# One step of a hybrid encoder layer: u in its own PSUM banks, the first sums of squares beside q and k, first scores behind a gate tile, two means ahead of the last chain

## The reference

```python
xn = rms_norm(x, g_mix)
h = xn @ w_in                       # [u | q | k | v | gate_a | gate_b]
gates = sigmoid(gates + b_gate)
y_pool = multiscale_pool(u)         # trailing windows 2/4/8/16, mean minus token, per-group map, scale
z = q k^T / 8                       # strictly causal
log_not = where(causal, log_sigmoid(-z), 0)
suffix = sum of log_not over the later keys
o = exp(log_sigmoid(z) + suffix) @ v          # stick-breaking, no softmax
x = x + (gate_a * (y_pool @ w_pool_up) + gate_b * (o @ w_sb_up)) @ w_out
x = x + square(relu(rms_norm(x) @ w_up)) @ w_down
x = x + sigmoid(rms_norm(x) @ w_ple_gate) * (p @ w_ple_proj)
y = rms_norm(x)                     # outputs also: k, v and the last 15 rows of u
```

## Time and profile before

| | |
|---|---|
| median of 3 runs | 793.26 us (792.95 to 793.46) |
| the profiled execution's own time | 793.77 us |
| its span | 791.9 us |
| PE busy | 773.7 us (98%) |
| DVE busy | 494.8 us (62%) |
| ACT busy | 381.5 us (48%) |
| POOL busy | 96.9 us (12%) |
| granted PE clock, mean | 0.996 |

### The profile page before, as it was taken

One profiled execution on the slowest core, in us unless ns is written; L12 is line 12 of the kernel. 1 busy time (PEld: TensorE's weight loads), 2 busy tenths in 40 slices (PEclk: granted clock), 3 DMA queues, 4 the chain that ended last, 5 costly groups with the idle time before them and its releaser, 6 DMA issues.

```text
span 791.9 us, 14329 instructions
## 1 busy us (share of the span) xinstructions
PE 773.7 (98%) x6050; PEld 765.2 (97%) x6050; DVE 494.8 (62%) x606; ACT 381.5 (48%) x443; POOL 96.9 (12%) x169
## 2 busy tenths in 40 slices
PE   8899999999999999999999999999999999999993
PEld 8899999999999899999999999999999999999993
DVE  5876566566566547787763367434763367677965
ACT  6554534535575443665641255213642155555643
POOL 1040140150150000020001100020001100100001
PEclk9999999999999999999999999999999999999998
DMA  7342231232221316786566847587575856826402
GB/s 236 99 125 74 70 120 53 82 105 56 98 90 55 107 54 206 240 202 178 179 171 168 202 160 206 139 188 183 158 192 145 204 171 180 195 82 161 119 1 113
DMA packets 33097, 110.18 MB, mean 139 GB/s; under 512 B 4496, under 2 KB 4496, under 8 KB 33040
## 3 DMA queue, kind: packets, MB, share of 16 engines
q1 hardware_dynamic: 24768, 84.72, 32.4%
q0 software_dynamic: 6016, 21.04, 14.9%
q10 hardware_dynamic: 2256, 3.60, 1.3%
HBM read 94.33 MB, written 4.52 MB: 125 GB/s over the span
## 4 chain that ended last, share of the span: by engine, by line
PE 90%; DVE 5%; ACT 2%; issue 1%; DMA 1%; SPq 1%; DVEq 0%; ACTq 0%
PE psum L1352 24%; PE psum L1061 19%; PE psum L1067 19%; PE psum L1064 19%; PE psum L1114 1%; DMA xt<-x_t 1%; PE psum L1042 1%; PE psum L1142 1%; PE psum L1043 1%; PE psum L1044 1%; PE psum L1140 1%; PE psum L1430 1%; PE psum L1102 1%; DVE work L1473 1%; PE psum L1101 1%
## 5 line engine op out<-in xcount | busy, mean ns | idle before, releaser
L699 ACT ACTIVATE w_hi<-raw_more 128x1024 fp32r<-128x1024 f32 x84 | 88.7, 1056 | 133.0 <-PE psum L1067 100.7
L1064 PE MATMUL psum<-b_lo,w_hi 128*128 128x272 f32 x688 | 142.0, 288 | 0.0
L1061 PE MATMUL psum<-b_hi,w_hi 128*128 128x272 f32 x672 | 139.3, 288 | 0.0
L1067 PE MATMUL psum<-b_hi,w_lo 128*128 128x272 f32 x672 | 138.8, 288 | 0.0
L1061 PE MATMUL psum<-a_hi,w_hi 128*128 128x272 f32 x576 | 120.8, 291 | 3.3 <-DVE a_lo L1462 1.2
L1456 DVE TENSOR_TENSOR w_lo<-raw_more,w_hi 128x1024 fp32r<-128x1024 f32 x84 | 102.2, 1222 | 34.6 <-ACT w_hi L699 34.3
L1067 PE MATMUL psum<-a_hi,w_lo 128*128 128x272 f32 x576 | 119.0, 288 | 0.0
L1064 PE MATMUL psum<-a_lo,w_hi 128*128 128x272 f32 x576 | 118.8, 288 | 0.0
L1352 PE MATMUL psum<-u_hi,w_hi 128*128 128x272 f32 x560 | 115.9, 288 | 0.2 <-ACT h_of L933 0.2
L1352 PE MATMUL psum<-u_hi,w_lo 128*128 128x272 f32 x560 | 115.7, 288 | 0.0
L1352 PE MATMUL psum<-u_lo,w_hi 128*128 128x272 f32 x560 | 115.5, 287 | 0.0
(11 more groups left out here) (245 smaller groups left out, 1010.3 us busy)
## 6 DMA issues: line engine op xcount, KB each, us to landing
raw_more<-w_tiles SPq DMA_DIRECT2D x84, 512.0 KB, 4.3
raw<-w_tiles SPq DMA_DIRECT2D x66, 512.0 KB, 3.5
raw_more<-w_tiles POOLq DMA_DIRECT2D x16, 512.0 KB, 6.7
raw_more<-raw_more POOLq DMA_DIRECT2D x14, 512.0 KB, 8.3
xt<-x_t SPq DMA_DIRECT2D x8, 272.0 KB, 6.2
y_t<-xt SPq DMA_DIRECT2D x8, 272.0 KB, 2.5
raw<-w_tiles POOLq DMA_DIRECT2D x4, 512.0 KB, 7.6
raw_more<-raw POOLq DMA_DIRECT2D x3, 512.0 KB, 6.4
```

What stands on the lines that cost most here:

```text
L699: act.activation(w_hi[:, t % W_RING, :, :].rearrange("p k c -> p (k c)"), src, ACT.Copy)\
L1061: pe.matmul(base[:, h, :], w_hi[:, s, wk, :], at(hi, k, h * HALF, (h + 1) * HALF), start=(opens and q == 0), stop=False, skip_group_check= ...
L1064: pe.matmul(base[:, h, :], w_hi[:, s, wk, :], at(lo, k, h * HALF, (h + 1) * HALF), start=False, stop=False, skip_group_check=True)
L1067: mm = pe.matmul(base[:, h, :], w_lo[:, s, wk, :], at(hi, k, h * HALF, (h + 1) * HALF), start=False, stop=(closes and q == len(ks) - 1), s ...
```

## The change

Pair 0 is written in a new order. `result_slot` gives u (tile 3) slot 3, banks 6 and 7. The sums of squares are made behind the fourth step of tile 2, not the second, as four matmuls of 136 columns in place of two of 272, into unused columns of banks 0 to 3. TensorE's order in pair 0 becomes tiles 0, 1, 2, 3, 4, scores of head 0, transposes of v, tiles 5 and 6, sums, tile 7, outputs of head 0, scores of head 1. Before it was tiles 0 to 3, scores, transposes, tiles 4 and 5, sums, tile 6, outputs, scores of head 1, tile 7. ScalarE and VectorE are reordered with it, and v's store is issued earlier on ScalarE. In the last pair the casts of means 2 and 3 stand before head 1's chain on ScalarE, behind a wait for that head's scores, and their low parts before the first pass on VectorE.

```diff
 def result_slot(n):
-    return (n if n < 3 else 0) if n < 4 else (n - N_ATT + 2) % 4 if n >= N_ATT else n % 2
+    return n if n < 4 else (n - N_ATT + 2) % 4 if n >= N_ATT else n % 2
...
+        first_sums = psum[:, 0:4, HALF:HALF + HALF // 2]
...
# ScalarE, pair(i)
-                if not first:
-                    prob(1, i - 1)
+                if first:
+                    split(AHEAD + 2)
+                    act.wait_ge(taken, 3)
+                    act.dma_start(v_t[i, :, :], ev[:, 2, 0:TOK]).then_inc(kv_out[1], 16)
+                    split(AHEAD + 3)
+                    split(AHEAD + 4)
+                    chain(0, i)
+                    values_hi(i)
+                    split(AHEAD + 5)
+                    stick_hi(0, i)
+                    split(AHEAD + 6)
+                    prob(0, i)
+                    split(AHEAD + 7)
+                    prob_hi(0, i)
+                    chain(1, i)
+                    stick_hi(1, i)
+                    return
+                prob(1, i - 1)
...
-                chain(1, i)
-                if last:
+
+                    act.wait_ge(z_done, HEADS)
                     mean_hi(2)
                     mean_hi(3)
+                chain(1, i)
...
# TensorE
-                if q == 1:
+                if q == 3:
                     pe.wait_ge(const_made, N_CONST)
                     pe.wait_ge(sq_added, KT)
-                    stats(None).then_inc(stat0, 1)
+                    for b in range(4):
+                        mm = pe.matmul(first_sums[:, b, :], negone[:, :].bitcast(F32),
+                                       acc[:, b * HALF // 2:(b + 1) * HALF // 2], start=True, stop=True)
+                    mm.then_inc(stat0, 1)
...
                     tile(3, i)
-                else:
-                    tile(0, i)
-                    tile(1, i)
-                    sums(1, i - 1)
-                    tile(2, i)
-                if first:
-
-                    pe.wait_ge(var_done, 1)
-                    pe.wait_ge(taken, 3)
-                else:
-                    outputs(1, i - 1)
+                    tile(4, i)
+
+                    pe.wait_ge(taken, 4)
+                    scores(0, i)
+                    v_rows(i)
+                    tile(5, i)
+                    tile(6, i)
+                    sums(0, i)
+                    tile(7, i)
+                    outputs(0, i)
+                    scores(1, i)
+                    return
...
# VectorE, pair(i)
+                pool_input(i)
                 if first:
+                    split(AHEAD + 3)
+                    split(AHEAD + 4)
+                    gate(0, i)
                     stick(0, i)
-                    split(AHEAD + 3)
                     stick_later(0, i)
+                    values_lo(i)
+                    split(AHEAD + 5)
+                    stick_lo(0, i)
+                    gate(1, i)
+                    split(AHEAD + 6)
+                    gate(2, i)
+                    split(AHEAD + 7)
+                    prob_lo(0, i)
+                    gate(3, i)
+                    head_out(0, i)
+                    stick(1, i)
+                    stick_later(1, i)
+                    stick_lo(1, i)
+                    return
...
                 if last:
                     group_lo(1)
+                    mean_lo(2)
+                    mean_lo(3)
                 else:
                     split(AHEAD + 7, i, S1_PER)
                 stick(1, i)
                 if last:
-                    mean_lo(2)
                     gate(3, i)
-                    mean_lo(3)
```

More of the change, by code:

```diff
@@ L798, in group_hi, with values_hi @@
                                scale=pscale[:, g:g + 1]).then_inc(ghi_done, 1)
+            def values_hi(i):
+                act.wait_ge(vt_done, i + 1)
+                act.activation(v_parts[:, :, V_HI, :], o_heads, ACT.Copy).then_inc(vhi_done, 1)
             def pair(i):
@@ L816, in pair @@
                 act.dma_start(k_t[i, :, :], ev[:, 1, 0:TOK]).then_inc(kv_out[0], 16)
-                if not first:
-                    prob(1, i - 1)
+                if first:
[16 more added lines that the diff above has]
+                prob(1, i - 1)
                 split(AHEAD + 2, i, S1_PER, 2)
-                if not first:
-                    prob_hi(1, i - 1)
+                prob_hi(1, i - 1)
                 chain(0, i)
@@ L1085, in tile @@
                 dense(pair_result(j, i), j % W_RING, ALL, A).then_inc(full, 1)
[L1087 to L1093, removed]
             def scores(hh, i):
@@ L1195, in pair @@
                     tile(3, i)
-                else:
-                    tile(0, i)
-                    tile(1, i)
-                    sums(1, i - 1)
-                    tile(2, i)
-                if first:
-                    pe.wait_ge(var_done, 1)
-                    pe.wait_ge(taken, 3)
-                else:
-                    outputs(1, i - 1)
+                    tile(4, i)
[9 more added lines that the diff above has]
+                    return
+                tile(0, i)
+                tile(1, i)
+                sums(1, i - 1)
+                tile(2, i)
+                outputs(1, i - 1)
                 scores(0, i)
-                if not first:
-                    tile(3, i)
+                tile(3, i)
                 v_rows(i)
@@ L1473, in add_square, with variance @@
                     dve.tensor_tensor(acc, acc, ev[:, 1 + k % 2, 0:TOK], ALU.add).then_inc(sq_added, 1)
[L1475 to L1481, removed]
+            def variance(sums, signal, parts=2):
+                dve.tensor_scalar(var.rearrange("p (a c) -> p a c", a=parts), sums, -1.0 / D_MODEL, EPS, ALU.mult,
+                                  ALU.add).then_inc(signal, 1)
             def root_step(nth):
@@ L1525, in _ @@
             dve.wait_ge(stat0, 1)
-            inverse_rms(psum[:, 6:8, 0:HALF], 1, var_done)
+            variance(first_sums, var_done, 4)
+            root_step(1)
             def stick(hh, i):
@@ L1568, in gate, with pool_input, values_lo @@
                    .then_inc(taken, 1)
+            def pool_input(i):
+                dve.wait_ge(full, 4 + i * S1_PER)
+                u = upad[:, i, :]
+                dve.tensor_tensor(u[:, U_PROMPT:U_PROMPT + HALF], pair_result(3, i)[:, 0, :], rn[:, 0:HALF], ALU.mult)
+                dve.tensor_tensor(u[:, U_PROMPT + HALF:U_STATE], pair_result(3, i)[:, 1, 0:SEQ - HALF],
+                                  rn[:, HALF:SEQ], ALU.mult)
+                dve.tensor_tensor(u[:, U_SAMPLE:PADW], pair_result(3, i)[:, 1, SEQ - HALF:HALF],
+                                  rn[:, SEQ:TOK], ALU.mult).then_inc(taken, 1)
+            def values_lo(i):
+                dve.wait_ge(vhi_done, i + 1)
+                dve.tensor_tensor(v_parts[:, :, V_LO, :], o_heads, v_parts[:, :, V_HI, :], ALU.subtract)\
+                   .then_inc(vlo_done, 1)
             def mean_lo(g):
@@ L1629, in pair @@
                     stick_later(0, i)
[L1631 to L1637, removed]
+                pool_input(i)
                 if first:
+                    split(AHEAD + 3)
+                    split(AHEAD + 4)
+                    gate(0, i)
                     stick(0, i)
-                    split(AHEAD + 3)
                     stick_later(0, i)
+                    values_lo(i)
[12 more added lines that the diff above has]
+                    return
                 stick_lo(0, i)
-                dve.wait_ge(vhi_done, i + 1)
-                dve.tensor_tensor(v_parts[:, :, V_LO, :], o_heads, v_parts[:, :, V_HI, :], ALU.subtract)\
-                   .then_inc(vlo_done, 1)
+                values_lo(i)
                 split(AHEAD + 4, i, S1_PER)
```

## The result

The changed kernel takes 796.39 us (median of 6 runs, 795.58 to 797.99), the one before 793.26 (6 runs on the same chip, 792.95 to 794.25). The ratio is 1.0041, with a 95% interval from 1.0031 to 1.0051. The profiled execution took 796.57 us, its span is 794.5, and its mean granted clock 0.993, where before had 0.996. How long the first loads take differs by about half a microsecond between runs, so in pair 0 I compare places by their distance from the start of tile 2 (T2): 21.14 us before, 20.67 after. A bracket in a row counts a wait from the modelled end of the work before it; counted from start to start, as the prediction counts, the same wait reads 0.15 to 0.2 us longer.

A forecast was written before the change was run, and what follows sets the result against it. TensorE, busy 773.7 of 791.9 us, was taken as the bound. Terms -0.69 + 2.83 - 0.36 gave +1.8 us on the median 793.26, so 795.0; own range 794.0 to 796.2, 8 in 10 within 793.2 to 796.5.

The forecast's parts named there:

- Sums of squares, d: Pair 0, tile 2: a 0.51 us wait is won, but all that follows rn comes d = 0.66 us later (0.5 to 1.1).
- Tile 4's weights: Pair 0: tile 4 waits for its low weight part, queued on VectorE behind rn and q; a new wait of 1.6 us.
- Sums(0,0): Pair 0, head 0's sums behind tile 6: they wait 0.55 us for VectorE's low parts, range 0 to 0.9.
- The long wait: First outputs after T10, outputs(1,0): TensorE waits 2.8 us, as the moved tile no longer covers VectorE's queue behind scores(1,0).
- rival A: Not slower: the wait at outputs(1,0) does not come; -1.05 us, 792.2; chance 0.12.
- The last pair: Last two means cast ahead of head 1's chain: third pool group stops waiting, fourth waits for the gate; 0.36 us won.
- rival C: TensorE's clock falls to 1.2 GHz after the wait at outputs(1,0), costing 3 us more: 798; chance 0.06.

The follow-up runs named there:

- The run with almost no wait: Changed kernel; in pair 1 head 1's probabilities made before k's high parts, their low part before tile 13's weight split (the probabilities ahead); 792.04 us, ratio 0.9988.
- the run with part 1 alone: Kernel before, with only the sums of squares moved behind tile 2's fourth step as four 136-column matmuls, u in its old banks; 794.57 us against 792.97.
- the one with tile 4's weights early: Changed kernel with tile 4's weights split before the norm's root instead of behind q; 794.78 us, ratio 1.0019 to the kernel before.

## Why the prediction was wrong: the chain of waits held, the clock did not

Forecast were +1.8 us and 795.0, with a range of its own from 794.0 to 796.2; measured are +3.1 and 796.4. Point by point, waits counted from start to start:

- **Sums of squares, d.** They started 3.01 behind T2's start, as forecast. The variance began at 4.13 behind it, 3.55 before: d = 0.58, forecast 0.66. Eight records of 136 columns end 1.09 after their start, four of 272 took 1.16: the narrower shape costs nothing.
- **Tile 4's weights.** 1.48 instead of 1.6 (1.33 in the row's bracket).
- **Sums(0,0).** 0.48 instead of 0.55; the masks took 1.04, as forecast. By sums(1,0) the change had won 0.84 against T2, forecast 0.69. Right.
- **The long wait.** 2.79 against 2.83. The chain was as written: q of T8 at 77.44, s + 12.30 (forecast s + 12.22), k at s + 17.20 (forecast 17.21), outputs at s + 24.56 (forecast 24.6), where s is 65.14. The run with almost no wait, 792.04, is near the price of rival A too, which I had at 792.2.
- **The last pair.** 0.54 instead of 0.36: the fourth group waits for the gate, as forecast; the third group came 0.45 earlier against its pair, not 0.36, and the pool projection 2.59 after it, not 2.67.
- **The failed step is rival C, the clock, which I left out of the sum.** The terms that I did count come to -0.84 + 2.79 - 0.54 = +1.41, near the +1.8. I had the clock at a chance of 0.06 and a price of 3. It came, at 1.68: far likelier than I had it, and at little more than half the price. The term "the wait costs what the wait lasts" should have read 2.79 + 1.68.

The error lies in how rows 13 were read. They show five idle microseconds at 1.00 behind the last matmul, from 780 to 785, and I took them for the clock's answer to any wait of that length. The window ends too early. The same trace goes on like this (us, PE busy (records), granted clock, DMA share, GB/s), and its page has the clock below 9 tenths in the last slice:

```profile
785.00:786.00 1.00, 0.00 (x0) 0.54 0.66 257
786.00:791.00 5.00, 0.00 (x0) 0.50 1.02 394
```

```profile
PEclk9999999999999999999999999999999999999998
```

TensorE's last matmul ends at 779.93, the clock falls at about 785.1, with TensorE idle all the while, and it stays at 0.50. So the trace that I had showed, 0.1 us past rows 13, that the clock does come down with TensorE idle, here some 5 us after it had stopped. Nor is 5 us a bound: in the run with the probabilities ahead the last matmul ends at 778.36 and the clock is at 0.50 from 781 on, at most 2.7 us later. In the changed kernel TensorE stops at 87.08, and the clock falls at about 90.6, some 3.5 us later, when TensorE is already at work again; a reading of the wait alone, 88 to 89, shows 1.00. A granted clock of 1.00 inside a gap does not say that the clock stays up behind it.

The Trainium skill ("TensorE: Matmul & The Clock Gate", "Why this matters for your kernels") asks for no gap above about 3 us between bursts of matmuls, and by that rule the waits of this case lay inside. Here the measurement differs: waits of 2.33 and 2.62 us brought the clock down in the traces, waits of 1.33 and 1.50 did not. Nothing between 1.50 and 2.33 was tried.

What stays open is why the same wait does not always do it. In the run with part 1 alone and in the one with tile 4's weights early, 6 of 21 executions have a clock and a time as if it had stayed up; no trace of such an execution was kept. The loss of the first of these is otherwise placed in its trace: it is 1.09 behind at sums(0,0) against T2, the longer wait and the slow clock in tile 3 less the old wait for u, which is gone; and 0.54 more at scores(1,0), where a new wait for the probabilities, 0.26 in its bracket, shows.

## What to carry to other kernels

When tiles of work are moved from one side of a phase to the other, price the side that loses them: the queue behind the moved tile had six microseconds less cover, and its chain of links, not the engine's busy share, set the end. A new wait of TensorE as long as those here (2.3 us and more) is to be priced with a stretch at half clock behind it (here 1.5 to 1.7 us more, in most executions), so a short piece taken out of such a chain can be worth more than twice its length. To judge whether a gap costs the clock, read the granted clock well past the gap, in the work behind it, and do not end the window where it still reads 1.00.

## What the runs showed of the hardware that I had not expected

- The clock falls late: it was still 1.00 all through a wait of 2.62 us and went to 0.50 in the microsecond after work had begun again, for about 3.4 us. Work beginning again is not what brings it down: behind the last matmul it fell as well, with nothing to run. A fill of 22 unread matmuls over the same wait kept it at 1.00.
- Waits of 2.33 and 2.62 us did not bring it down in every execution: in 6 of 21 runs the mean granted clock stayed at 0.994 or 0.995 and the run was 1.1 to 1.5 us shorter.
- GpSimd's four masks took 1.03 us beside a VectorE instruction that reads one operand from PSUM, and 2.75 beside three with both operands in SBUF, one after the other.
